# Attention with filler work placed by a table, and a first projection copied by ScalarE

## The chip, the cores and the metric

The kernel runs on all 8 cores of one Trainium2 chip. Each core computes one of the 8 batch elements by itself, and the cores exchange nothing. The metric is the time in microseconds (us) of the slowest core for one execution, lower being better. The engines of a core are TensorE (PE in the profile, with PEld for its weight loads), VectorE (DVE), ScalarE (ACT), GpSimd (POOL) and SyncE (SP). TensorE writes its results to PSUM, which the program divides into eight banks of 128 x 512 float32.

## The reference

Two layers, each a half-weighted SwiGLU, a mixer and another half-weighted SwiGLU, all with RMS norms and residual additions. The change touches only the mixer of layer 0, a banded attention with 16 heads of 64:

```
q, k, v = jnp.split(h @ w_in, 3, axis=-1)
q = rms_norm(q.reshape(b, nc, CHUNK, N_HEADS, HEAD_DIM), q_gain)
k = rms_norm(k.reshape(b, nc, CHUNK, N_HEADS, HEAD_DIM), k_gain)
scores = einsum('bnqhd,bnkhd->bnhqk', q, k_band) * HEAD_DIM ** -0.5
scores = where(valid, scores + bias, MASK_VALUE)
probs = softmax(scores)
out = einsum('bnhqk,bnkhd->bnqhd', probs, v_band).reshape(b, s, d)
return out @ w_out
```

Each chunk of 64 frames attends to itself and to the 8 chunks before it. A core has 2048 frames of width 1024.

## The kernel before

The activations lie transposed in on-chip memory: 8 row blocks of 128 channels by 2048 frames, the frames cut in 4 tiles (t) of 512. The program is six subprograms in a row: SwiGLU, attention, SwiGLU, SwiGLU, recurrent block, SwiGLU. Every engine has one queue, filled in the order in which the Python code records operations, and a small planner adds the semaphore waits that reads and writes need, per tile and per PSUM bank. So the order of the recorded calls is the order of the work, and an instruction that waits holds back all that was recorded after it on its engine.

**Pairs and steps.** Attention works on 8 pairs of heads (i = 0 to 7), a pair filling 128 channels. For a pair there are 28 steps: the tile t = 0 of queries meets 4 key blocks of 128, the tiles 1 to 3 meet 8 each, and a step spans 512, 384, 256 or 128 queries. `stage1(g)` computes the scores of step g for both heads into banks 0 and 1 or 2 and 3 (by turns), ScalarE takes the exponential of both into a buffer, and VectorE multiplies by the bias table and clears the corner outside of the band. `stage2(g - 2)` comes two steps later (LA = 2): four matmuls add values times probabilities in bank 4 and the row sums in bank 5. At the last step of a tile, ScalarE takes logarithm and exponential of bank 5, VectorE copies bank 4 and multiplies.

**Filler work.** Between stage1 and stage2 of the steps of pair i, the projections of pair i + 1 are put, since TensorE would have little to do otherwise. `proj_chunks` makes the list. `P1` is a projection of queries (`which` 0, bank 6) or keys (`which` 1, bank 7) of one tile: 8 matmuls of 512 columns in two halves of 4, then a copy to `raw` by VectorE (L672) and a square by GpSimd (L310). `P2` is the norm of a tile: two matmuls (`P2s`) sum the squares into banks 6 and 7, `P2f` takes one logarithm and one exponential over both banks (128 x 1024), and VectorE multiplies twice. `V` makes the values of two pairs for 128 frames: 8 matmuls of 256 columns into bank 6 or 7, then two casts by VectorE (L712). The list runs tile by tile: four halves of P1, up to two V, P2, then the other V. The loop over steps takes pieces from it by weight: each piece has a weight (0.87 or 0.6), each step has one by its columns (1.5 more at a tile's start), and pieces are taken while their share is not above that of the steps. What is left is issued at the next pair's first step. In pair 6 there are no V, and pair 7 has pieces of the output projection.

**First projection.** Pair 0's own projection overlaps the end of the SwiGLU before it. `seq0` lists 8 (tile, which) couples. For each of the first six, the sums of the one before (`after(x - 1)`) are issued first, into the same banks 0 to 3 that the projections use, then the whole P1. The rest follows with 16 V in banks 4 and 5, whose copies and casts are VectorE's.

`conv_bias` (two exponentials on ScalarE, a clear on VectorE, the next bias table's load on SP) comes at a pair's first step. Weights of a later pair are loaded from the GpSimd queue by `load_pair`.

Of the kernel before, what the change touches and what calls it, by code (L numbers as in the profile page):

```python
# [9 lines left out]
ALU = mybir.AluOpType  # L10
# [12 lines left out]
TAILJ = 20  # L23

ENGS = ("pe", "act", "dve", "pool", "sp")

class T:
    __slots__ = ("name", "last_w", "readers")
# [164 lines left out]
class Builder:  # L193
# [406 lines left out]
    def attention(self, n):  # L600
# [61 lines left out]
        def P1(p, t, which, bank, half=None):  # L662
            s = wsl(p)
            r = t % 2
            w = self.WA[s].rearrange("p (k m) -> p k m", k=8)
            tsl = slice(t * TT, (t + 1) * TT)
            for kc in (range(NCH) if half is None else range(4 * half, 4 * half + 4)):
                self.mm(bank, self.psum[bank], w[:, kc, which * 128:(which + 1) * 128], self.hT[:, kc, tsl],
                        kc == 0, kc == NCH - 1, [self.WA_t[s], self.h_t[kc][t]])
            if half == 0:  # L670
                return
            P.op("dve", lambda e: e.tensor_copy(out=raw[r][:, which, :], in_=self.psum[bank]),  # L672
                 reads=[self.ps_t[bank]], writes=[raw_t[r][which]])
            sqb, sqt = (E[2][:, which, :], sq0_t[which]) if p == 0 else (self.sq[which], self.sq_t[which])
            self.tt(sqb, raw[r][:, which, :], raw[r][:, which, :], ALU.mult,
                    [raw_t[r][which]], [sqt], eng="pool")

        def P2s(p, t, which, bank):
            sqb, sqt = (E[2][:, which, :], sq0_t[which]) if p == 0 else (self.sq[which], self.sq_t[which])
# [19 lines left out]
        def V(p, kt, bank):  # L699
            sa, sb = wsl(p), wsl(p + 1)  # L700
            lo, hi = min(sa, sb), max(sa, sb)
            d = hi - lo
            t = kt // 4
            ksl = slice(kt * 128, (kt + 1) * 128)
            for kc in range(NCH):
                self.mm(bank, self.psum[bank][:, 0:256], self.hT[:, kc, ksl],
                        WAall[:, lo:hi + 1:d, kc * 384 + 256:kc * 384 + 384], kc == 0, kc == NCH - 1,
                        [self.WA_t[sa], self.WA_t[sb], self.h_t[kc][t]])
            va, vb = p % NV, (p + 1) % NV
            order = (va, vb) if lo == sa else (vb, va)  # L710
            for j, sl in enumerate(order):
                P.op("dve", lambda e, j=j, sl=sl: e.tensor_copy(out=Vall[:, sl, kt, :], in_=self.psum[bank][:, j * 128:(j + 1) * 128]),  # L712
                     reads=[self.ps_t[bank]], writes=[v_t[sl][kt]])

        def proj_chunks(i):
            p = i + 1
            out = []
            vp, vk = None, []
            if i % 2 == 0 and i + 3 < 8:
                vp, vk = i + 2, list(range(0, 8))  # L720
            elif i % 2 == 1 and i + 2 < 8:
                vp, vk = i + 1, list(range(8, 16))
            nv = [0, 2, 3, 3]
            j = 0
            for t in range(NT):
                for which in range(2):
                    for half in range(2):
                        out.append((0.87, lambda t=t, which=which, half=half: P1(p, t, which, 6 + which, half)))
                mine = vk[j:j + nv[t]]
                j += nv[t]  # L730
                for kt in mine[0:2]:
                    out.append((0.87, lambda kt=kt: V(vp, kt, 6 + kt % 2)))
                out.append((0.6, lambda t=t: P2(p, t, 6)))
                for kt in mine[2:]:
                    out.append((0.87, lambda kt=kt: V(vp, kt, 7)))
            if p + 3 < 8:
                out.append((0.0, lambda: load_pair(p + 3)))
            return out

        seq0 = [(t, which) for t in range(NT) for which in range(2)]  # L740

        def after(x):
            t, which = seq0[x]
            P2s(0, t, which, 2 * (t % 2))
            if which == 1:
                P2f(0, t, 2 * (t % 2))

        for x in range(6):
            t, which = seq0[x]
            yield t  # L750
            if x == 0:
                load_pair(2)
            if x >= 1:
                after(x - 1)
            P1(0, t, which, 2 * (t % 2) + which)
        yield 99
        conv_bias(0)
        V(0, 0, 4)
        V(0, 1, 5)
        after(5)  # L760
        for kt in range(2, 8):
            V(0, kt, 4 + kt % 2)
        P1(0, 3, 0, 2)
        V(0, 8, 4)
        V(0, 9, 5)
        after(6)
        P1(0, 3, 1, 3)
        for kt in range(10, 14):
            V(0, kt, 4 + kt % 2)
        after(7)  # L770
        V(0, 14, 4)
        V(0, 15, 5)
        load_pair(3)

        out_w = [None] * 8
# [76 lines left out]
                self.tt(attnT[:, i, tsl], Osb, rsn, ALU.mult, [Osb_t, rsn_t], [at_t[i][t]])  # L852

        LA = 2
        fill = []
        done, total = 0.0, 0.0
        pend = []
        wgt = []
        for (t, kt, first, last) in seq:
            wgt.append(max(0.3, (min(TT * t + TT, 128 * kt + 640) - max(TT * t, 128 * kt)) / 512.0))  # L860
        for k in range(LA, ns):
            if seq[k - LA][2] and k > LA:
                wgt[k] += 1.5
        cum = [sum(wgt[:k + 1]) for k in range(ns)]
        for g in range(len(steps) + LA):
            i = g // ns
            k = g % ns
            if k == 0 and i < 8:
                while fill:
                    fill.pop(0)[1]()  # L870
                if i < 7:
                    conv_bias(i + 1)
            if g < len(steps):
                stage1(g)
            if k == LA and i < 8:
                if i < 7:
                    fill = proj_chunks(i)
                    total = sum(f[0] for f in fill)
                done = 0.0
                if i == 6:  # L880
                    for j in (0, 1, 2, 3, 6, 7):
                        load_out_w(j)
                if i == 7:
                    for j in (4, 5):
                        load_out_w(j)
            if i < 7:
                goal = total * (cum[k] - cum[LA - 1]) / (cum[ns - 1] - cum[LA - 1]) if k >= LA else 0.0
                while fill and done + fill[0][0] * 0.5 <= goal:
                    done += fill[0][0]
                    fill.pop(0)[1]()  # L890
            else:
                for _ in range(2):
                    if pend:
                        pend.pop(0)()
            if g >= LA:
                stage2(g - LA)
                i2, t2, kt2, first2, last2 = steps[g - LA]
                if i2 == 7 and last2 and t2 < 2:
                    for c in range(NCH):
                        for half in range(2):  # L900
                            pend.append(lambda t=t2, c=c, half=half: out_chunk(t, c, 6 + c % 2, half))
# [426 lines left out]
```

How the kernel before makes its waits and increments, by code:

```python
            def run(e, eng):  # L120
# [15 lines left out]
                    best = {}  # L136
                    for sem, val in waits:
                        k = id(sem)
                        if k not in best or best[k][1] < val:
                            best[k] = (sem, val)
                    waits = list(best.values())
                    embed = None
                    if waits and not op.is_dma:
                        embed = waits.pop()
                    for sem, val in waits:
                        eng.wait_ge(sem, val)
                    ins = op.fn(eng)
                    if embed is not None:
                        ins._wait_ge(embed[0], embed[1])
                    if op.is_dma:
                        ins.then_inc(dsem[op.dma_sem_id], 16)
                    elif op.needs_inc:
                        ins.then_inc(esem[e], 1)
                if e == "sp":
                    for op in final_wait_ops:
                        if waited_d[op.dma_sem_id] < op.dma_val:
                            eng.wait_ge(dsem[op.dma_sem_id], op.dma_val)
                            waited_d[op.dma_sem_id] = op.dma_val
```

## Time and profile before

| | us |
|---|---|
| three runs | 2743.55, 2738.2, 2742.05 (median 2742.05) |
| profiled execution, its own time | 2738.65 |
| its span, slowest core (core 4) | 2737.1 |
| spans of the eight cores | 2720.6 to 2737.1 |

The profile is one execution, seen on core 4; times count from the first instruction of that core. A row such as `PE ps L294 <- ACT arena L303` says that matmuls, all recorded at line 294, stood idle until an instruction of ScalarE, recorded at line 303, ended. Many lines are those of helpers (L294 matmul, L303 activation, L306 and L310 VectorE arithmetic, L310 on POOL the squares), so shapes tell what an instruction is. "Busy" of TensorE has its ends modelled. PEclk is the granted TensorE clock as a share of 2.4 GHz; half is 1.2 GHz. On this time axis attention runs from about 500 us to 990 us.

### The profile page before, as it was taken

The numbers are of one execution on the slowest core, as the hardware profiler recorded it, in microseconds if no ns is written. First come the engines' busy times: TensorE is split into PE (matmuls) and PEld (weight loads), VectorE is DVE, ScalarE is ACT, GpSimd is POOL, SyncE is SP. The second block draws the span as 40 slices with busy tenths as digits, with TensorE's granted clock in tenths as the row PEclk, the third lists the DMA queues.
The fourth block names the chain that finished last, engine by engine and source line by source line (L and its number), as shares of the span: only waits on it lengthen the run. The fifth ranks groups of instructions, "written<-read, shape, count | busy, mean of one in ns | idle before, by whom it ended". The sixth has DMA issues, their size and how long they took to land.

```text
span 2737.1 us, 30678 instructions; the slowest of 8 cores (2720.6 to 2737.1 us)
## 1 busy us (share of the span) xinstructions
PE 2567.1 (94%) x12224; PEld 1114.7 (41%) x12224; DVE 1179.1 (43%) x1851; ACT 789.9 (29%) x1141; POOL 347.9 (13%) x340
## 2 busy tenths in 40 slices
PE   6999999788888799999999999999978889999999
PEld 2444444333333234444444444444423334444444
DVE  4234234455555453423425243243567853424423
ACT  5110113255556542011014101102356632010010
POOL 0100000111111101000000100000048630000000
PEclk9999999899999899999999999999989999999999
DMA  6521310111001103231221412211111113222223
GB/s 151 85 38 25 54 28 15 27 32 16 16 16 21 30 1 61 37 54 28 34 35 16 74 27 43 45 29 28 20 21 20 18 27 61 40 50 32 34 35 119
DMA packets 56095, 105.85 MB, mean 39 GB/s; under 512 B 4624, under 2 KB 5776, under 8 KB 55952
## 3 DMA queue, kind: packets, MB, share of 16 engines
q0 software_dynamic: 44288, 83.90, 18.6%
q1 hardware_dynamic: 11664, 19.99, 2.5%
q8 instruction: 96, 1.57, 0.2%
q14 instruction: 47, 0.39, 0.0%
HBM read 179.37 MB, written 8.39 MB: 69 GB/s over the span
## 4 chain that ended last, share of the span: by engine, by line
PE 85%; DVE 6%; ACT 5%; POOL 2%; DMA 1%; issue 1%; SPq 0%; ACTq 0%; POOLq 0%; DVEq 0%
PE ps L294 85%; ACT arena L303 4%; DVE arena L306 3%; POOL arena L310 2%; DVE arena L310 1%; DMA arena<-xT 1%; DVE arena L317 1%; DVE arena L672 0%; SPq L332 0%; DVE arena L314 0%; DMA arena<-attn_wout 0%; ACT L303 0%; POOL arena L317 0%; DVE arena L850 0%; DMA arena<-lru_wout 0%
## 5 line engine op out<-in xcount | busy, mean ns | idle before, releaser
L294 PE MATMUL ps<-arena 128*128 128x512 bf16 (+6 forms) x12224 | 2567.1, 376 | 166.5 <-ACT arena L303 50.2
L294 PEld LDWEIGHTS ps<-arena 128*128 128x128 bf16 (+2 forms) x12224 | 1114.7, 100 | 1618.4 <-issue 222.3
L303 ACT ACTIVATE arena<-ps 128x512 bf16<-128x512 f32 (+5 forms) x680 | 444.9, 661 | 1698.3 <-PE ps L294 1653.7
L310 DVE TENSOR_TENSOR arena<-arena,ps 128x512 bf16<-128x512 bf16 x352 | 241.9, 688 | 951.6 <-PE ps L294 950.8
L306 DVE SCALAR_TENSOR_TENSOR arena<-ps,arena 128x512 f32<-128x512 f32 (+1 forms) x560 | 415.3, 742 | 222.6 <-PE ps L294 220.5
L303 ACT ACTIVATE arena<-arena 128x512 bf16<-128x512 f32 (+4 forms) x322 | 229.0, 742 | 160.2 <-PE ps L294 58.1
L310 POOL TENSOR_TENSOR arena<-arena 128x512 bf16<-128x512 f32 (+2 forms) x112 | 195.3, 1754 | 368.0 <-PE ps L294 258.5
L448 POOL DMA_DIRECT2D arena<-ffn_win x88 | 62.5, 710 | 1253.6 <-PE ps L294 1226.9
L306 DVE SCALAR_TENSOR_TENSOR arena<-arena,ps 128x512 bf16<-128x512 f32 x192 | 133.9, 742 | 33.7 <-ACT ps L303 33.7
L310 DVE TENSOR_TENSOR arena<-arena 128x512 bf16<-128x512 bf16 (+3 forms) x188 | 86.6, 473 | 91.9 <-ACT arena L303 90.0
L454 POOL DMA_DIRECT2D arena<-ffn_wout x88 | 48.5, 557 | 396.7 <-PE ps L294 396.1
L306 DVE SCALAR_TENSOR_TENSOR arena<-arena 128x512 bf16<-128x512 f32 (+3 forms) x88 | 57.2, 681 | 67.2 <-ACT arena L303 66.4
L303 ACT ACT_TABLE_LOAD x51 | 65.4, 1283 | 7.3 <-PE ps L294 3.5
L310 DVE TENSOR_TENSOR arena<-ps,arena 128x512 f32<-128x512 f32 x64 | 43.3, 689 | 51.7 <-PE ps L294 51.3
L303 ACT ACTIVATE arena<-ps,arena 128x512 f32<-128x512 f32 x64 | 43.8, 688 | 63.2 <-PE ps L294 63.2
L672 DVE COPY arena<-ps 128x512 f32<-128x512 f32 x64 | 43.4, 687 | 20.4 <-PE ps L294 19.6
L317 DVE TENSOR_SCALAR arena<-ps,arena 128x1024 f32<-128x1024 f32 x16 | 21.4, 1339 | 36.7 <-PE ps L294 23.1
L314 DVE TENSOR_SCALAR arena<-arena 128x1024 f32<-128x1024 f32 (+3 forms) x24 | 29.4, 1224 | 17.5 <-ACT arena L303 16.3
L712 DVE CAST arena<-ps 128x128 bf16<-128x128 f32 x128 | 29.9, 275 | 12.7 <-PE ps L294 12.1
L1081 DVE TENSOR_TENSOR_SCAN arena<-arena 128x1024 f32<-128x1024 f32 x8 | 31.8, 3975 | 0.8
L832 DVE MEMSET arena<- 64x128 bf16 x96 | 15.8, 165 | 36.3 <-ACT arena L303 33.8
L317 POOL TENSOR_SCALAR arena<-arena 128x1024 f32<-128x1024 f32 x16 | 21.1, 1319 | 60.3 <-ACT arena L303 60.2
(20 smaller groups left out, 87.6 us busy)
## 6 DMA issues: line engine op xcount, KB each, us to landing
arena<-ffn_win POOLq DMA_DIRECT2D x88, 512.0 KB, 5.3
arena<-ffn_wout POOLq DMA_DIRECT2D x88, 256.0 KB, 6.0
arena<-xT SPq DMA_DIRECT2D x32, 256.0 KB, 13.1
outT<-arena SPq DMA_DIRECT2D x32, 256.0 KB, 2.9
arena<-attn_win POOLq DMA_DIRECT2D x8, 768.0 KB, 7.8
arena<-lru_win POOLq DMA_DIRECT2D x8, 512.0 KB, 5.3
arena<-bias_tab SPq DMA_DIRECT2D x8, 256.0 KB, 4.3
arena<-attn_wout POOLq DMA_DIRECT2D x8, 256.0 KB, 4.8
```

The source lines that it names most:

```text
L294: self.P.op("pe", lambda e: e.matmul(out_ap, lhsT, rhs, start=start, stop=stop), reads=reads, writes=[self.ps_t[bank]])
L303: self.P.op("act", lambda e: e.activation(out=out, in_=in_, func=func, **kw), reads=reads, writes=writes)
L306: self.P.op("dve", lambda e: e.scalar_tensor_tensor(out=out, in0=in0, scalar=scalar, in1=in1, op0=op0, op1=op1), reads=reads, writes=writes)
L310: self.P.op(eng, lambda e: e.tensor_tensor(out=out, in0=in0, in1=in1, op=op), reads=reads, writes=writes)
L314: self.P.op(eng, lambda e: e.tensor_scalar(out=out, in0=in0, scalar1=s1, scalar2=None, op0=op0), reads=reads, writes=writes)
L317: self.P.op(eng, lambda e: e.tensor_scalar(out=out, in0=in0, scalar1=s1, scalar2=s2, op0=op0, op1=op1), reads=reads, writes=writes)
L448: P.dma("pool", lambda e: e.dma_start(out=self.WA[s][:, 0:2048], in_=self.fwin_d[fi, j], max_dma_last_dim=4096), self.WA_sem[s], writes=[s ...
L454: P.dma("pool", lambda e, s=s, j=j: e.dma_start(out=self.WBall[:, s, :], in_=self.fwout_d[fi, j * 128:(j + 1) * 128, :], max_dma_last_dim= ...
L672: P.op("dve", lambda e: e.tensor_copy(out=raw[r][:, which, :], in_=self.psum[bank]), reads=[self.ps_t[bank]], writes=[raw_t[r][which]])
L712: P.op("dve", lambda e, j=j, sl=sl: e.tensor_copy(out=Vall[:, sl, kt, :], in_=self.psum[bank][:, j * 128:(j + 1) * 128]), reads=[self.ps_t ...
L832: P.op("dve", lambda e: e.memset(E[r][0:64, :, 576 - lo:640 - lo], 0.0), reads=Ex_t[r], writes=et)
L1081: P.op("dve", lambda e: e.tensor_tensor_scan(out=hb, data0=tha, data1=thx, initial=carry[:, 0:1], op0=ALU.mult, op1=ALU.add), reads=[that, ...
```

## The change

Four edits. First, `PLAN` takes the place of the weights: a table with a row for even and one for odd pairs, with 28 entries each. An entry lists the pieces issued at that step between stage1 and stage2. Letters: `q21` is the second half of P1 for the queries of tile 2, `k` the same for keys; `s` and `t` are the sum matmul of queries and of keys of a tile; `f` and `g` are the rest of their norms; `v37` is V number 3 in bank 7. Second, the norm is cut in two: `F` takes the logarithm in place in its bank, the exponential from the bank to `rs`, and multiplies, each over 512 columns, for queries and keys apart. So a pair has 40 pieces: 16 halves, 8 sums, 8 norm parts, 8 V. Third, in the first projection the copies and casts go from VectorE to ScalarE, sums go to banks 4 and 5, V to banks 6 and 7, and the sums of couple x - 2 are issued between the two halves of couple x. Last, `load_pair` is at the start of the following pair's first step, where it had been the last piece of the list.

```diff
--- before.py
+++ after.py
@@ -23,6 +23,23 @@
 TAILJ = 20
 
 ENGS = ("pe", "act", "dve", "pool", "sp")
+
+PLAN = [
+    ["", "k00 q00", "q01 k01", "",
+     "", "s0 t0 f0 g0", "q10 q11 k10", "k11",
+     "", "", "s1 t1 f1", "g1",
+     "q20 q21", "", "k20 k21 v06", "",
+     "", "s2 v17 f2", "t2 g2 v46", "",
+     "", "v37", "q30 q31 k30 k31", "v26",
+     "", "s3 v77 f3", "", "v56 t3 v66 g3",],
+    ["", "q00 q01 k00 k01", "s0 f0", "",
+     "t0 q10 q11 g0", "", "k10 k11", "",
+     "", "", "s1 t1 f1 g1", "",
+     "q20 q21", "v17", "v06 k20", "",
+     "k21", "s2 f2", "", "v27 v36",
+     "", "t2 v46", "q30 g2 q31", "k30 k31",
+     "s3 v77 f3", "v57", "", "t3 v66 g3",],
+]
 
 class T:
     __slots__ = ("name", "last_w", "readers")
@@ -669,11 +686,13 @@
                         kc == 0, kc == NCH - 1, [self.WA_t[s], self.h_t[kc][t]])
             if half == 0:
                 return
-            P.op("dve", lambda e: e.tensor_copy(out=raw[r][:, which, :], in_=self.psum[bank]),
-                 reads=[self.ps_t[bank]], writes=[raw_t[r][which]])
+            if p == 0:
+                self.act(raw[r][:, which, :], self.psum[bank], AF.Copy, [self.ps_t[bank]], [raw_t[r][which]])
+            else:
+                P.op("dve", lambda e: e.tensor_copy(out=raw[r][:, which, :], in_=self.psum[bank]),
+                     reads=[self.ps_t[bank]], writes=[raw_t[r][which]])
             sqb, sqt = (E[2][:, which, :], sq0_t[which]) if p == 0 else (self.sq[which], self.sq_t[which])
-            self.tt(sqb, raw[r][:, which, :], raw[r][:, which, :], ALU.mult,
-                    [raw_t[r][which]], [sqt], eng="pool")
+            self.tt(sqb, raw[r][:, which, :], raw[r][:, which, :], ALU.mult, [raw_t[r][which]], [sqt], eng="pool")
 
         def P2s(p, t, which, bank):
             sqb, sqt = (E[2][:, which, :], sq0_t[which]) if p == 0 else (self.sq[which], self.sq_t[which])
@@ -709,67 +728,75 @@
             va, vb = p % NV, (p + 1) % NV
             order = (va, vb) if lo == sa else (vb, va)
             for j, sl in enumerate(order):
-                P.op("dve", lambda e, j=j, sl=sl: e.tensor_copy(out=Vall[:, sl, kt, :], in_=self.psum[bank][:, j * 128:(j + 1) * 128]),
-                     reads=[self.ps_t[bank]], writes=[v_t[sl][kt]])
-
-        def proj_chunks(i):
+                if p == 0:
+                    self.act(Vall[:, sl, kt, :], self.psum[bank][:, j * 128:(j + 1) * 128], AF.Copy, [self.ps_t[bank]], [v_t[sl][kt]])
+                else:
+                    P.op("dve", lambda e, j=j, sl=sl: e.tensor_copy(out=Vall[:, sl, kt, :], in_=self.psum[bank][:, j * 128:(j + 1) * 128]),
+                         reads=[self.ps_t[bank]], writes=[v_t[sl][kt]])
+
+        def F(p, t, which):
+            r = t % 2
+            bank = 6 + which
+            tsl = slice(t * TT, (t + 1) * TT)
+            self.act(self.psum[bank], self.psum[bank], AF.Ln, [self.ps_t[bank]], [self.ps_t[bank]], scale=1.0, bias=64.0 * EPS)
+            self.act(self.rs[which], self.psum[bank], AF.Exp, [self.ps_t[bank]], [self.rs_t[which]], scale=-0.5)
+            dst, dst_t, sc, sc_t = (qT, q_t, qg, self.cv_t) if which == 0 else (kT, k_t, kg8, self.dc_t)
+            self.stt(dst[p % 2][:, tsl], raw[r][:, which, :], sc, self.rs[which], ALU.mult, ALU.mult,
+                     [raw_t[r][which], self.rs_t[which], sc_t], [dst_t[p % 2][t]])
+
+        def token(i, tok):
             p = i + 1
-            out = []
-            vp, vk = None, []
-            if i % 2 == 0 and i + 3 < 8:
-                vp, vk = i + 2, list(range(0, 8))
-            elif i % 2 == 1 and i + 2 < 8:
-                vp, vk = i + 1, list(range(8, 16))
-            nv = [0, 2, 3, 3]
-            j = 0
-            for t in range(NT):
-                for which in range(2):
-                    for half in range(2):
-                        out.append((0.87, lambda t=t, which=which, half=half: P1(p, t, which, 6 + which, half)))
-                mine = vk[j:j + nv[t]]
-                j += nv[t]
-                for kt in mine[0:2]:
-                    out.append((0.87, lambda kt=kt: V(vp, kt, 6 + kt % 2)))
-                out.append((0.6, lambda t=t: P2(p, t, 6)))
-                for kt in mine[2:]:
-                    out.append((0.87, lambda kt=kt: V(vp, kt, 7)))
-            if p + 3 < 8:
-                out.append((0.0, lambda: load_pair(p + 3)))
-            return out
+            kind = tok[0]
+            if kind in "qk":
+                which = "qk".index(kind)
+                P1(p, int(tok[1]), which, 6 + which, int(tok[2]))
+            elif kind in "st":
+                which = "st".index(kind)
+                P2s(p, int(tok[1]), which, 6)
+            elif kind in "fg":
+                F(p, int(tok[1]), "fg".index(kind))
+            elif kind == "v":
+                n_, b_ = int(tok[1]), int(tok[2])
+                if i % 2 == 0 and i + 3 < 8:
+                    V(i + 2, n_, b_)
+                elif i % 2 == 1 and i + 2 < 8:
+                    V(i + 1, 8 + n_, b_)
 
         seq0 = [(t, which) for t in range(NT) for which in range(2)]
 
         def after(x):
             t, which = seq0[x]
-            P2s(0, t, which, 2 * (t % 2))
+            P2s(0, t, which, 4)
             if which == 1:
-                P2f(0, t, 2 * (t % 2))
+                P2f(0, t, 4)
 
         for x in range(6):
             t, which = seq0[x]
             yield t
             if x == 0:
                 load_pair(2)
-            if x >= 1:
-                after(x - 1)
-            P1(0, t, which, 2 * (t % 2) + which)
+            P1(0, t, which, 2 * (t % 2) + which, 0)
+            if x >= 2:
+                after(x - 2)
+            P1(0, t, which, 2 * (t % 2) + which, 1)
         yield 99
+        V(0, 0, 6)
+        after(4)
+        V(0, 1, 7)
+        V(0, 2, 6)
+        after(5)
         conv_bias(0)
-        V(0, 0, 4)
-        V(0, 1, 5)
-        after(5)
-        for kt in range(2, 8):
-            V(0, kt, 4 + kt % 2)
+        for kt in range(3, 6):
+            V(0, kt, 6 + kt % 2)
         P1(0, 3, 0, 2)
-        V(0, 8, 4)
-        V(0, 9, 5)
+        P1(0, 3, 1, 3)
+        V(0, 6, 6)
         after(6)
-        P1(0, 3, 1, 3)
-        for kt in range(10, 14):
-            V(0, kt, 4 + kt % 2)
+        V(0, 7, 7)
+        V(0, 8, 6)
         after(7)
-        V(0, 14, 4)
-        V(0, 15, 5)
+        for kt in range(9, 16):
+            V(0, kt, 6 + kt % 2)
         load_pair(3)
 
         out_w = [None] * 8
@@ -852,31 +879,17 @@
                 self.tt(attnT[:, i, tsl], Osb, rsn, ALU.mult, [Osb_t, rsn_t], [at_t[i][t]])
 
         LA = 2
-        fill = []
-        done, total = 0.0, 0.0
         pend = []
-        wgt = []
-        for (t, kt, first, last) in seq:
-            wgt.append(max(0.3, (min(TT * t + TT, 128 * kt + 640) - max(TT * t, 128 * kt)) / 512.0))
-        for k in range(LA, ns):
-            if seq[k - LA][2] and k > LA:
-                wgt[k] += 1.5
-        cum = [sum(wgt[:k + 1]) for k in range(ns)]
         for g in range(len(steps) + LA):
             i = g // ns
             k = g % ns
-            if k == 0 and i < 8:
-                while fill:
-                    fill.pop(0)[1]()
-                if i < 7:
-                    conv_bias(i + 1)
+            if k == 0 and 0 < i < 8 and i + 3 < 8:
+                load_pair(i + 3)
+            if k == 0 and i < 7:
+                conv_bias(i + 1)
             if g < len(steps):
                 stage1(g)
             if k == LA and i < 8:
-                if i < 7:
-                    fill = proj_chunks(i)
-                    total = sum(f[0] for f in fill)
-                done = 0.0
                 if i == 6:
                     for j in (0, 1, 2, 3, 6, 7):
                         load_out_w(j)
@@ -884,10 +897,8 @@
                     for j in (4, 5):
                         load_out_w(j)
             if i < 7:
-                goal = total * (cum[k] - cum[LA - 1]) / (cum[ns - 1] - cum[LA - 1]) if k >= LA else 0.0
-                while fill and done + fill[0][0] * 0.5 <= goal:
-                    done += fill[0][0]
-                    fill.pop(0)[1]()
+                for tok in PLAN[i % 2][k].split():
+                    token(i, tok)
             else:
                 for _ in range(2):
                     if pend:
```

## Rows read from the trace of the kernel before

**Rows 1.** the profile's page, its first engine row and the chain that ended last

```profile
PE 2567.1 (94%) x12224; PEld 1114.7 (41%) x12224; DVE 1179.1 (43%) x1851; ACT 789.9 (29%) x1141; POOL 347.9 (13%) x340
PE 85%; DVE 6%; ACT 5%; POOL 2%; DMA 1%; issue 1%; SPq 0%; ACTq 0%; POOLq 0%; DVEq 0%
```

**Rows 2.** windows: length; PE, PEld, DVE, ACT, POOL busy (count); granted clock

```profile
503.00:557.70 54.70, 38.71 (x206) 21.12 (x204) 23.77 (x56) 12.75 (x16) 9.12 (x9) 0.84 0.03 6
...
665.70:720.30 54.60, 46.69 (x304) 18.87 (x304) 28.95 (x73) 32.53 (x47) 9.02 (x9) 0.94 0.22 35
...
884.20:943.00 58.80, 43.68 (x242) 13.49 (x242) 27.97 (x59) 34.28 (x48) 11.05 (x13) 0.84 0.12 19
960.00:1700.00 740.00, 735.34 (x3451) 326.13 (x3450) 280.57 (x424) 149.24 (x243) 44.34 (x71) 1.00 0.23 38
```

**Rows 3.** waits of the matmuls, 560 to 890 us (total, times, longest)

```profile
PE ps L294 <- ACT arena L303: 24.2, 24, 1.2
PE ps L294 <- POOL arena L310: 8.0, 6, 1.4
PE ps L294 <- DVE arena L672: 7.5, 6, 1.2
PE ps L294 <- DVE arena L850: 4.0, 6, 1.5
PE ps L294 <- DVE arena L310: 3.2, 6, 0.5
PE ps L294 <- DVE arena L712: 1.3, 6, 0.2
```

**Rows 4.** timeline of TensorE in pair 1 (start, us, ..., idle before)

```profile
622.37 0.38 PE L294 MATMUL ps<-arena 128*128 128x512 bf16 x1 [1.37 <-POOL arena L310]
...
655.87 5.42 PE L294 MATMUL ps<-arena 128*128 128x256 bf16 x42 [1.25 <-DVE arena L672]
```

**Rows 5.** windows of one us in pair 1

```profile
621.00:622.00 1.00, 0.01 (x1) 0.00 (x0) 0.73 (x2) 0.97 (x3) 0.81 (x1) 1.00 0.00 0
...
623.00:624.00 1.00, 0.14 (x1) 0.11 (x2) 0.11 (x1) 0.97 (x2) 0.00 (x0) 1.00 0.00 0
624.00:625.00 1.00, 1.00 (x3) 0.30 (x2) 0.07 (x1) 0.90 (x1) 0.00 (x0) 0.50 0.00 0
```

**Rows 6.** ScalarE's groups by shape in pair 2, 665.7 to 720.3 us

```profile
L303 ACT ACTIVATE arena<-ps 128x1024 bf16<-128x1024 f32 x8 | 8.0, 1019 | 2.8 <-PE ps L294 2.0 <-DVE arena L310 0.5 <-DVE arena L832 0.3
...
L303 ACT ACTIVATE arena<-arena 128x1024 f32<-128x1024 f32 x4 | 4.2, 1058 | 0.1
...
L303 ACT ACTIVATE arena<-ps 128x1024 f32<-128x1024 f32 x4 | 4.1, 1021 | 0.3 <-PE ps L294 0.2
L303 ACT ACTIVATE arena<-ps 128x256 bf16<-128x256 f32 x7 | 2.7, 379 | 4.3 <-PE ps L294 3.2 <-DVE arena L310 1.1
...
L303 ACT ACTIVATE arena<-ps 128x512 f32<-128x512 f32 x4 | 2.4, 598 | 2.1 <-PE ps L294 2.1
```

**Rows 7.** timeline of TensorE in the first projection (first and fifth of five gaps)

```profile
506.61 2.10 PE L294 MATMUL ps<-arena 128*128 128x512 bf16 x9 [1.56 <-POOL arena L310]
...
528.22 5.54 PE L294 MATMUL ps<-arena 128*128 128x512 bf16 x25 [2.68 <-POOL arena L310]
```

**Rows 8.** waits of the matmuls, 884.2 to 943 us

```profile
PE ps L294 <- POOL arena L310: 7.2, 3, 3.1
```

**Rows 9.** timeline of GpSimd in pair 1, a square

```profile
621.18 1.04 POOL L310 TENSOR_TENSOR arena<-arena 128x512 bf16<-128x512 f32 x1 [1.45 <-PE ps L294]
```

**Rows 10.** VectorE's groups by shape in pair 2

```profile
L672 DVE COPY arena<-ps 128x512 f32<-128x512 f32 x8 | 5.4, 687 | 1.4 <-PE ps L294 1.3
...
L712 DVE CAST arena<-ps 128x128 bf16<-128x128 f32 x16 | 3.7, 272 | 1.2 <-PE ps L294 1.1
```

**Rows 11.** timeline of ScalarE before the first projection

```profile
488.41 1.28 ACT L303 ACT_TABLE_LOAD   x1
489.70 0.60 ACT L303 ACTIVATE arena<-ps 128x512 f32<-128x512 f32 x1
```


## Prediction

> **What bounds the kernel now.** I read the page first. TensorE is busy 94% of the span and holds 85% of the chain that ended last [rows 1], so time can only come from TensorE's idle time or its clock. The windows by stage then say where both are [rows 2]. In the SwiGLU from 960 us TensorE is busy 735.34 of 740 us at a granted clock of 1.00: nothing to win. In attention, one steady pair takes 54.6 us with 46.69 busy, so 7.9 idle, at clock 0.94. Pair 0 takes 53.3 us and the other five to 884.2 us all take 54.6 or 54.7 with the same counts (304 matmuls), so one pair stands for six. The first projection (503 to 557.7 us) has 38.71 busy of 54.7 at 0.84, and pair 6 with the head of pair 7 (884.2 to 943) has 43.68 busy of 58.8 at 0.84.
>
> The waits say what each idle piece is [rows 3]. Between 560 and 890 us they sum to 24.2 + 8.0 + 7.5 + 4.0 + 3.2 + 1.3 = 48.2 us, or 8.0 a pair, and come in fixed numbers: four a pair on ScalarE, one each on the others. The timeline gives the place [rows 4]. The first tile's sums follow its last projection at once and wait 1.37 us for the square of GpSimd. Right behind, the next projection wants bank 6 and waits some 1.0 us (24.2 by 24 [rows 3]) until the logarithm over both banks has read it. Later a V waits 1.25 us for the copy out of its bank. These are waits of order, not of load: ScalarE is busy 32.53, VectorE 28.95 and GpSimd 9.02 of 54.6 us [rows 2].
>
> Last, the clock. It falls to 1.2 GHz (0.50) twice a pair, both times behind the pair's start with its short steps and waits, the second time at 624 us; from 621 to 624 us TensorE was nearly idle (0.01 and 0.14 busy in two of the three microseconds) [rows 5]. A mean of 0.94 over 54.6 us is 0.06 x 54.6 = 3.3 us of lost full-speed work. So a steady pair is 46.7 - 3.3 = 43.4 us of work at 2.4 GHz, 3.3 of clock and 7.9 idle.
>
> **The change, part by part.**
>
> *The table in pairs 0 to 5.* It removes and adds no matmul. What moves: sums now come one to five steps behind their projection, and the norm parts one or more steps before the next use of their bank. I walked the queues with the rows' durations. The norm was 1.02 + 1.06 = 2.08 us of ScalarE for a tile; now it is four instructions of 512 columns at 0.60 (the nearest row, 598 ns, reads a bank and writes on-chip memory; in place no row shows) = 2.4, so 0.3 more a tile, 1.3 a pair [rows 6]. ScalarE then has 33.8 us of a pair, below TensorE's 43.4, but every exponential of scores queued behind an F comes 1.2 us later. The cover is LA = 2: stage2 wants it two steps later, with the filler of two steps between (9 matmuls of 512 columns take 2.10 us to their end [rows 7], so a half projection, or a V with its 8 of 256, is some 0.9).
>
> Even row, step 5 ("s0 t0 f0 g0") is the tight place. The scores of step 4 end at 0 on my count, those of step 5 at 0.9; their exponentials (1.02 each) end at 1.0 and 2.0, f0 at 3.2, g0 at 4.4. TensorE has the two sums, stage2 of step 3 and the scores of step 6 until about 1.9, and the next piece, q10, wants bank 6: a wait of 1.3 us. I found only 0.3 more there (t0 for the square of k) and no other in the even row: s1, s2, s3 and the V that follow have at least one step between. In the odd row, f0 and g0 are at steps 2 and 4, and my count gives 0.4 us at s0 and 0.4 at the copy of bank 4. At the pair's boundary the old order had the norm (2.08), the two bias exponentials (1.0) and the step's exponential in one run before the second step's scores; now g3 alone (1.2) is there, behind a V. So 1.6 and 0.8 us by the walk; semaphore delays and VectorE's own queue are not in it, so I take 2.2 idle a pair. From below it can't be less than 0, from above it is today's 7.9 if every wait only changes its name.
>
> With no idle piece above 1.4 us in a row, the stretch that pulled the clock down is gone: waits such as the 1.25 us at 655.87 [rows 4], alone in their surroundings, were not followed by a fall. I take 0.6 us for clock losses left, between 0 and today's 3.3. A pair is then 43.4 + 2.2 + 0.6 = 46.2 us, a gain of 8.4, or 50 for six; the bounds are 0 and 11.2 a pair.
>
> *Pair 6.* Work at full clock in the 58.8 us: the lost clock is 0.16 x 58.8 x 0.74 (the busy share) = 7.0, so 43.7 - 7.0 = 36.7, and 15.1 idle, of which 7.2 are three waits for the square (one 3.1 us long) because no V stands between P1 and P2 [rows 8]. The table keeps the distance in steps though the V are gone, so these go. But ScalarE has 34.28 + 1.3 = 35.6 us there, nearly TensorE's own work, so steps without filler run at ScalarE's pace, above all 16 to 21. I take 9 idle and 5 of clock: 50.7, a gain of 8, taken as 7; bounds 0 and 15.
>
> *First projection.* Five gaps, all but one for the square, 11.0 us in sum (1.56, 2.22, 2.41, 2.12, 2.68; first and last in [rows 7]), come from `after(x - 1)` ahead of P1(x). With `after(x - 2)` between halves the square has 1.73 + 0.9 = 2.6 us, against a copy of 0.6 and a square of 1.04 [rows 9], so four of them go; the one behind a P2f waits some 0.2 us as the copy is now queued on ScalarE behind 2.08 us of norm. A copy on ScalarE costs 0.60 for 0.69 on VectorE [rows 6, 10]; a cast of 128 columns shows on no ScalarE row: between 0 and the 0.38 of 256 columns, I take 0.27, for 0.27 on VectorE. New is that V's casts stand behind norm and bias exponentials on ScalarE (1.02 + 1.06 + 1.0 = 3.1 us) while only two banks serve V (1.76 us of TensorE): 1.3 to 1.9 us of waiting after after(5), and about 0.9 after after(7). Work at full clock is 38.7 - 0.16 x 54.7 x 0.71 = 32.5; with 5.5 idle and 4 of clock it is 42.0, a gain of 12.7, taken as 10 because this part has most unseen operations; bounds -3 (all gaps stay, and the 2.8 of V are added) and 17.
>
> The Trainium skill (ScalarE: Activation LUTs, Table sets) says that cheap functions, copy among them, are in every table set. By it the copies need no table load, which is the sum above. The trace bears it out only for its kin: after the load at 488.41 us, logarithm, exponential and square run mixed without another [rows 11]. If copy wanted a set of its own, each switch would cost the 1.28 us of that row, and with ten groups of copies between the norms, so 20 switches, the first projection would be 26 us longer and the time about 2700.
>
> *Loads.* `load_pair` stays at the pair boundary; first use of its weights is 14 steps later, over 20 us, so nothing hangs on it. SP has only the bias table, which is asked for at the same step.
>
> **Sum.** 50 + 7 + 10 = 67 us off the profiled execution's own 2738.65, which is 2672. That execution lies 3.4 below the median of the runs shown, so the forecast is about 2674.
>
> **The rivals.**
>
> *A, the forecast:* the waits go and the clock follows. 2655 to 2695. Chance 0.58.
>
> *B, half of it:* the waits go by half, since VectorE's queue (multiply behind exponential, then the raw copy behind that) moves later what my walk has in time, and the clock falls as often as now. 4 a pair, 6 in the first projection, 3 in pair 6: 24 + 6 + 3 = 33, so 2708; span 2695 to 2725. For it: ScalarE and VectorE are each busy more than half of a pair [rows 2], and each works strictly in the recorded order. Against it: the slack of two steps. 0.21.
>
> *C, new waits for old:* bank 6 and 7 are held through F's exponential, where they were free after the logarithm, and every tile pays as step 5 does. Four tiles by 1.3 and a longer start leave 1 us a pair or less: 2735 to 2745, so 2738. 0.08.
>
> *D, the other side, ScalarE's queue:* eight F a pair put 1.2 us each ahead of a score exponential. If the next stage2 has no filler to cover them, TensorE pays 8 x 1.2 = 9.6 a pair where 7.9 went, 1.7 x 6 = 10, and 3 in the first projection: 2755. It decides from the point where more than six of the eight F are uncovered; the even row has two in a step at step 5 only, and my walk finds one uncovered. 0.10.
>
> *E, a limit on dense work:* a denser TensorE is granted less. With the clock staying where it is and only the idle gone, 5.7 x 6 + 5 + 7 = 46 remain, 2696. The Trainium skill (TensorE: Matmul & The Clock Gate, Part 1) speaks against the change here: it says that once three cores of a die run dense matmuls the die is held to 13/16. By it the densest stretches could not have full clock. This case's trace disagrees: 99% busy at 1.00 for 740 us, with eight cores at work [rows 2]. 0.03.
>
> **How the numbers follow.** The likeliest is A, 2674. Leaving out the slower side and most of C, which is 2 in 10, the range is 2652 to 2722; its lower end is 90 off the profiled time (with the 3.4 of the median), nine tenths of what the upper bounds give together (67 + 15 + 17 = 99). About 0.2% (5.5 us) is what a measurement can tell from no change. Faster by more: A, B, E and a little of C, 0.85. Same: 0.06. Slower: D and the tail of C, 0.09.
>
> **What would show it.** Right: a steady pair of 45 to 48 us with under 3.5 idle, its clock at 0.98 or more; no wait for POOL in it; a wait on ScalarE of 1.0 to 1.6 us in even pairs only, before q10; 503 to the first score in 40 to 46 us with no new ACT_TABLE_LOAD; and the stretches after attention as before. Wrong: pairs above 50 us, waits of VectorE's copies that my walk has in time, or a clock that still falls behind each pair's start.

## The result and the profile after

The changed kernel takes 2652.5 us (median), the kernel before 2742.05, so 89.5 us less; the ratio is 0.9677, 95% interval 0.9655 to 0.9699, or 3.2% less. Forecast were 2674 with a range of 2652 to 2722. At times one die ran slower whatever the kernel; every number here is from undisturbed runs.

The page of the kernel after, its engine row and its chain, for [rows 1]:

```profile
PE 2530.7 (95%) x12224; PEld 1113.0 (42%) x12224; DVE 1175.0 (44%) x1811; ACT 800.3 (30%) x1237; POOL 349.4 (13%) x340
PE 89%; DVE 6%; ACT 2%; DMA 1%; issue 1%; POOL 1%; SPq 0%; ACTq 0%; DVEq 0%; POOLq 0%
```

The same matmuls (x12224) are 36 us less busy, and idle time fell by 50. The windows of the stages, for [rows 2] (length; busy us of the engines; granted clock). The first is the first projection, then pairs 0 and 1, pairs 0 to 5 together, and pair 6:

```profile
498.00:543.00 45.00, 41.55 (x254) 23.79 (x253) 20.57 (x31) 26.51 (x62) 9.52 (x9) 1.00 0.11 23
543.00:586.10 43.10, 41.23 (x298) 18.30 (x297) 29.08 (x70) 31.99 (x53) 9.01 (x9) 1.00 0.25 44
586.10:631.40 45.30, 42.95 (x306) 18.83 (x305) 30.18 (x73) 32.26 (x55) 9.23 (x9) 1.00 0.02 7
...
543.00:809.80 266.80, 254.49 (x1819) 112.33 (x1818) 180.06 (x430) 195.17 (x323) 54.93 (x54) 1.00 0.13 24
809.80:862.00 52.20, 42.03 (x268) 14.67 (x265) 29.14 (x63) 35.92 (x60) 12.91 (x16) 0.89 0.20 29
```

Six pairs that took 326.5 us (557.7 to 884.2) take 266.8, or 44.5 each, and the clock is 1.00 where it was 0.94. The waits of the matmuls in these 266.8 us, for [rows 3]:

```profile
PE ps L311 <- DVE arena L734: 5.2, 12, 0.8
PE ps L311 <- DVE arena L877: 2.9, 6, 0.6
PE ps L311 <- ACT arena L320: 2.5, 3, 1.5
PE ps L311 <- POOL arena L327: 1.3, 2, 0.7
```

That is 11.9 us where there were 48.2, and the 24 waits for ScalarE became three. The largest part of what is left (5.2) is for VectorE's casts of V out of their bank (L734): in odd pairs k20 and q30 come close behind a V in their bank (0.43 and 0.78 us), and in each two pairs a V does so twice (0.37 and 0.15). In TensorE's timeline of the pairs the longest stretches without a gap were 16.6 us; now one is 32.7, and two things stand out (start, us, ..., idle before), for [rows 4, 7]:

```profile
526.74 9.30 PE L311 MATMUL ps<-arena 128*128 128x256 bf16 x66 [1.84 <-ACT arena L320]
536.95 12.26 PE L311 MATMUL ps<-arena 128*128 128x256 bf16 x88 [0.91 <-ACT arena L320]
550.71 32.72 PE L311 MATMUL ps<-arena 128*128 128x512 bf16 x236 [1.50 <-ACT arena L320]
...
639.93 32.72 PE L311 MATMUL ps<-arena 128*128 128x512 bf16 x236 [0.51 <-ACT arena L320]
...
820.97 0.58 PE L311 MATMUL ps<-arena 128*128 128x512 bf16 x1 [5.19 <-POOL arena L327]
```

The first two are the V of the first projection, the next two are q10 behind step 5 of even pairs, and the last is new: 5.19 us in pair 6. GpSimd's queue tells why:

```profile
812.12 1.59 POOL L812 DMA_DIRECT2D arena<-attn_wout  x3 [6.75 <-PE ps L311]
819.23 0.53 POOL L812 DMA_DIRECT2D arena<-attn_wout  x1 [5.52 <-DMA arena<-attn_wout]
819.77 2.05 POOL L327 TENSOR_TENSOR arena<-arena 128x512 bf16<-128x512 f32 x2
```

Row block 7 of the output weights goes to another part of the buffer of row block 6, but the planner tracks that buffer as one. So its load waits 5.52 us for the landing of block 6, and two squares stand behind it. Behind the idle time the clock is 0.50 from 820 to 826 us. Of the unseen operations, the logarithm in place takes what I assumed (first line, 545 to 803 us), and so does the cast (second, 498 to 543 us):

```profile
L320 ACT ACTIVATE ps<-ps 128x512 f32<-128x512 f32 x46 | 27.4, 595 | 2.2 <-PE ps L311 2.2
...
L320 ACT ACTIVATE arena<-ps 128x128 bf16<-128x128 f32 x32 | 6.8, 276 | 5.4 <-PE ps L311 5.4
```

The time axis of a trace starts with its core's first instruction, and what lies ahead of attention differs by some us between cores: the ScalarE table load just ahead of the first projection is at 488.41 us in the trace before [rows 11] and 4.5 later in this one. So stages are best counted between marks inside one trace. The marks here are that load, the weight load of the first score (first line after, second before), and VectorE's copies of bank 4 at the end of pairs 5 and 6:

```profile
492.95 1.28 ACT L320 ACT_TABLE_LOAD   x1
...
541.42 0.12 PEld L311 LDWEIGHTS ps<-arena 64*128 64x128 bf16 x4 [0.21 <-issue]
...
555.39 0.11 PEld L294 LDWEIGHTS ps<-arena 64*128 64x128 bf16 x4 [0.21 <-issue]
```

| us between the marks | before | after | e1 | e2 | e3 | e10 |
|---|---|---|---|---|---|---|
| load to first score | 67.0 | 48.5 | 67.0 | 49.1 | 49.1 | 48.5 |
| first score to end of pair 5 | 330.7 | 270.3 | 272.3 | 330.6 | 308.1 | 302.7 |
| end of pair 5 to end of pair 6 | 56.2 | 45.7 | 46.0 | 55.9 | 47.9 | 47.7 |

From before to after that is 18.5 + 60.4 + 10.5 = 89.4 us, all of the measured difference, and behind pair 6 the two traces are as long to 1.2 us (1794.8 and 1793.6). The first row before differs by core, from 65.6 (core 7) to 68.1 (core 2), while after it is 48.5 on all of cores 0, 2, 3, 5 and 7, so the 18.5 stands for some 17 to 20. The other columns are the runs of the next section.

### The profile page after: what moved, and what is told of

Its sections match the earlier page's. It is cut to its first block, busy times and chain, and to the rows that moved or that the text cites. A ratio compares the mean times of both kernels' runs of the same rounds, so it can differ in the third digit from the quotient of the medians.

```text
span 2651.0 us, 30732 instructions; the slowest of 8 cores (2646.7 to 2651.0 us)
## 1 busy us (share of the span) xinstructions
PE 2530.7 (95%) x12224; PEld 1113.0 (42%) x12224; DVE 1175.0 (44%) x1811; ACT 800.3 (30%) x1237; POOL 349.4 (13%) x340
## 4 chain that ended last, share of the span: by engine, by line
PE 89%; DVE 6%; ACT 2%; DMA 1%; issue 1%; POOL 1%; SPq 0%; ACTq 0%; DVEq 0%; POOLq 0%
PE ps L311 89%; DVE arena L323 4%; ACT arena L320 2%; DVE arena L334 1%; DMA arena<-ffn_win 1%; DVE arena L327 0%; POOL arena L327 0%; DMA arena<-xT 0%; DVE arena L331 0%; DMA arena<-lru_wout 0%; DMA arena<-attn_wout 0%; SPq L349 0%; DVE arena L877 0%; DVE arena L734 0%; ACT ps L320 0%
## 5 line engine op out<-in xcount | busy, mean ns | idle before, releaser
L311 PE MATMUL ps<-arena 128*128 128x512 bf16 (+6 forms) x12224 | 2530.7, 373 | 116.7 <-ACT arena L320 26.4
L320 ACT ACTIVATE arena<-ps 128x512 bf16<-128x512 f32 (+6 forms) x748 | 457.2, 626 | 1602.2 <-PE ps L311 1580.0
L320 ACT ACTIVATE arena<-arena 128x512 bf16<-128x512 f32 (+4 forms) x294 | 199.0, 710 | 154.3 <-PE ps L311 58.2
L327 DVE TENSOR_TENSOR arena<-arena 128x512 bf16<-128x512 bf16 (+3 forms) x188 | 92.6, 505 | 55.9 <-ACT arena L320 52.2
L320 ACT ACTIVATE ps<-ps 128x512 f32<-128x512 f32 x56 | 33.4, 596 | 6.6 <-PE ps L311 6.6
L1092 DVE TENSOR_TENSOR_SCAN arena<-arena 128x1024 f32<-128x1024 f32 x8 | 31.8, 3977 | 0.8
L1087 DVE TENSOR_TENSOR_SCAN arena<-arena 128x1024 f32<-128x1024 f32 x8 | 25.0, 3122 | 5.7 <-POOL arena L327 5.7
```

The lines of the kernel that those rows point to most:

```text
L311: self.P.op("pe", lambda e: e.matmul(out_ap, lhsT, rhs, start=start, stop=stop), reads=reads, writes=[self.ps_t[bank]])
L320: self.P.op("act", lambda e: e.activation(out=out, in_=in_, func=func, **kw), reads=reads, writes=writes)
L327: self.P.op(eng, lambda e: e.tensor_tensor(out=out, in0=in0, in1=in1, op=op), reads=reads, writes=writes)
L1087: P.op("dve", lambda e: e.tensor_tensor_scan(out=hb, data0=tha, data1=thx, initial=0.0, op0=ALU.mult, op1=ALU.add), reads=[that, thxt], wr ...
L1092: P.op("dve", lambda e: e.tensor_tensor_scan(out=hb, data0=tha, data1=thx, initial=carry[:, 0:1], op0=ALU.mult, op1=ALU.add), reads=[that, ...
```

## The experiments

**The two halves by themselves.** First the table with the first projection as before (`e1_table_only`), then the new first projection with the old list (`e2_first_projection_only`).

```diff
# e1, on the kernel after
-            if p == 0: self.act(raw..., AF.Copy, ...)      # V's casts likewise
+            P.op("dve", ... tensor_copy ...)
-            P2s(0, t, which, 4)
+            P2s(0, t, which, 2 * (t % 2))
...  # the loop over seq0 and the V after it as in the kernel before
# e2: the reverse, on the kernel before
```

> The table and the split norm, with the first projection as it was (copies and casts on VectorE, sums in banks 0 to 3, V in 4 and 5, sums of the couple before ahead of each projection). The theory: the parts add up, so the 13.8 us of the first projection stay and the 60.6 of pairs 0 to 5 and 10.5 of pair 6 go: about 2668 us, ratio to before 0.973 to 0.975, a steady pair 44.6 us at clock 1.00. Rival: the pairs are this fast only because VectorE starts them without a backlog and TensorE enters them at full clock; then the ratio is 0.98 or more and the first pairs take over 47 us.

> Only the first projection is changed; the list, its weights and the joint norm stay. The theory: 13.8 us less, about 2728 us, ratio 0.995, pairs still 54.6 us at clock 0.94. [...]

Measured: e1 2672.0 us, ratio 0.9756 (0.9737 to 0.9776), 67 less than before. e2 2720.9, ratio 0.9936 (0.9916 to 0.9955), 18 less. The sum, 85, is the whole within the intervals, so the parts are nearly independent. Of e1's rival 2 us are true: with the casts on VectorE the six pairs take 272.3 us in place of 270.3, in e1 as in `e7_casts_on_vector` below. In e2 the pairs kept their length and a clock of 0.94 (542 to 868 us). e2 gave more than the 13.8 I had read off the start of pair 0, because I had compared two time axes that are 4.5 us apart; between marks it is 17.9 in e2 and 18.5 in the changed kernel.

**The cut of the norm.** Once taken back in the changed kernel (`e3_table_joint_norm`), once alone in the kernel before (`e4_list_split_norm`), once cut but kept together (`e10_cut_together`).

```diff
# e3, in token(), on the kernel after
-                P2s(p, int(tok[1]), which, 6)
+                if which == 1: P2(p, int(tok[1]), 6)       # s, f, g: nothing
# e4, in P2, on the kernel before
-            P2f(p, t, bank)
+            F(p, t, 0); F(p, t, 1)
# e10: as e3, with both P2s, F(p, t, 0), F(p, t, 1) at t
```

> The changed kernel, but the norm of a tile is in one piece again, as before: both sums, one logarithm and one exponential over 1024 columns and both multiplies are issued at the table's entry t. Theory (the distance in steps does it, not the cut): ScalarE has 0.3 us less a tile, and a wait of about 1 us comes only where a q follows t at once (odd pairs, tile 0): 2650 to 2668 us, ratio to before 0.967 to 0.973. Rival (the cut of the norm does it, since long logarithms no longer stand before the scores' exponentials): over 2690 us, ratio above 0.98.

> The kernel before with the norm cut in two as in the change, all else as before. Theory: bank 6 is free after logarithm and exponential of 512 (1.2 us) where it was free after one logarithm of 1024 (1.02), so the wait grows by 0.2 us for each of 28 tiles and ScalarE by 0.3: 2742 to 2752 us, ratio 1.000 to 1.004. Rival (the cut does it): under 2720 us, ratio below 0.992.

> As the run with the joint norm (both sums and the whole norm at the table's entry t), but with the norm cut in two: logarithm and exponential of 512 for queries, then for keys, back to back. It parts the cut from the distance. If the 37 us that the joint norm cost come from the pieces now standing together at t (bank 6 asked for right behind), cutting them gives little: 2680 to 2700 us, ratio to before 0.978 to 0.985. If the long instructions do it, it is near the changed kernel: under 2665 us, ratio below 0.972.

Measured: e3 2690.3 us, a single run and so without an interval, some 38 more than the changed kernel; e4 ratio 1.0008 (0.9997 to 1.0019); e10 2686.4 in its profiled execution, with a wide ratio, 0.9856 (0.9784 to 0.9927). On e3 my theory, 2650 to 2668, missed, and the number lies at the edge of the rival's (over 2690). But what the rival says, that the cut itself does it, fell by e4 and e10: cutting gives nothing in the old list, and 4 to 5 us with the pieces together (the six pairs take 302.7 us in e10, 308.1 in e3). What counts is that a cut norm can be put apart: that is 32 us of the six pairs (302.7 to 270.3), while the table with an uncut norm gives 23 (330.7 to 308.1). A window and the waits of e3 from 560 to 800 us:

```profile
560.00:800.00 240.00, 210.78 (x1436) 90.20 (x1434) 136.95 (x342) 150.66 (x216) 43.06 (x42) 0.96 0.10 20
```

```profile
PE ps L311 <- ACT arena L320: 17.2, 14, 1.9
PE ps L311 <- DVE arena L734: 5.6, 10, 0.7
```

Fourteen waits for ScalarE of up to 1.9 us are back (the changed kernel has two, 1.0 us in all, in this stretch), and with them falls of the clock (0.96 for 1.00). By the table's order, a projection or V right behind t asks for bank 6 before the long logarithm has read it.

**Does idle time pull the clock down?** `e5_idle_filled` puts matmuls that nobody reads into two waits of each pair of the kernel before.

```diff
+            if k == 2 and i < 7: dummy(4)                  # ahead of stage1
+        def dummy(n): n matmuls, ones x hT[:, 0, 0:512], into bank 6
         def P2(p, t, bank):
+            if t == 0: dummy(5)
```

> The kernel before, with extra matmuls (ones times 512 columns of the input, into bank 6, never read) inside two waits of each pair: 5 before the sums of tile 0, where TensorE waits 1.4 us for the square, and 4 before the scores of the third step, where it waits 1.2 us. They do no useful work and lengthen no chain by more than 0.3 us. If idle time is what pulls the clock down, one or both falls of a pair go and with them 1.7 to 3.4 us a pair: 2720 to 2732 us, ratio 0.992 to 0.997, clock of a pair 0.97 to 1.00. Rival: the falls belong to the kind of work at the pair's start (short steps, 64 rows); then the clock stays 0.94 and the time is the same or up to 4 us longer (ratio 1.000 to 1.002).

Measured: 2722.8 us, ratio 0.9936 (0.9917 to 0.9956): 17 us less with 63 more matmuls. A window of exactly one pair, and the wait for the square in two pairs one after the other:

```profile
671.22:722.90 51.68, 44.82 (x309) 19.01 (x314) 29.43 (x73) 32.60 (x47) 9.01 (x9) 1.00 0.13 21
```

```profile
671.22 0.38 PE L294 MATMUL ps<-arena 128*128 128x512 bf16 x1 [0.32 <-POOL arena L310]
...
722.90 0.38 PE L294 MATMUL ps<-arena 128*128 128x512 bf16 x1 [0.44 <-POOL arena L310]
```

A pair is 51.68 us in place of 54.6, and both falls are gone although the short steps stand where they were. So it is the idle time before a fall that does it. Without the nine added matmuls (1.9 us, at the 735.34 us for 3451 of [rows 2]) the pair has 42.9 us of work, or up to 43.8 since four of its 313 matmuls are missing from the trace, where it had 46.69. So the falls cost 2.9 to 3.8 us a pair; the prediction read 3.3 from 0.94. The rival (the kind of work) fell.

**How near is ScalarE's queue?** `e8_exp_twice` does each norm part's exponential twice.

```diff
             self.act(self.rs[which], self.psum[bank], AF.Exp, ..., scale=-0.5)
+            self.act(self.rs[which], self.psum[bank], AF.Exp, ..., scale=-0.5)
```

> The changed kernel with the exponential of each norm part done twice (same result): 0.60 us more of ScalarE, 8 times a pair in 7 pairs, 33.6 us in all. It asks how much slack the queue has. Theory (norm parts are covered by filler, LA = 2): most of it is hidden, up to 12 us longer, ratio to before 0.968 to 0.973. Rival (ScalarE's queue is on the path, as in my case of the other side): 25 us or more, ratio above 0.977.

Measured: 2672.6 us, ratio 0.9755 (0.9738 to 0.9771), some 20 more than the changed kernel of the 33.6 added. Between both expectations: the queue has slack for the work as it is, and of 0.6 us more a norm part it hides about two fifths. Its waits from 560 to 800 us:

```profile
PE ps L311 <- ACT arena L320: 10.5, 19, 1.0
PE ps L311 <- POOL arena L327: 4.1, 8, 1.4
```

**Mending what is left.** `e6_late_load` moves one load; `e7_casts_on_vector` takes the casts of the first projection back to VectorE; `e11_four_banks` gives its V four banks; `e12_both_mends` is e6 and e11.

```diff
# e6
-                    for j in (0, 1, 2, 3, 6, 7):
+                    for j in (0, 1, 2, 3, 6):
+            if i == 6 and k == 19: load_out_w(7)
# e7, in V
-                if p == 0: self.act(Vall..., AF.Copy, ...)
+                P.op("dve", ... tensor_copy ...)
# e11, after the loop over seq0: banks of the V
-        6, 7, 6 | 7, 6, 7 | 6, 7, 6 | 7, 6, 7, 6, 7, 6, 7
+        6, 7, 0 | 1, 6, 7 | 0, 1, 6 | 7, 0, 1, 6, 7, 6, 7
```

> The changed kernel with one load moved: row block 7 of the output weights, which shares a buffer with row block 6 and so waits on the GpSimd queue for that load's landing, ahead of two squares in pair 6, is issued at step 19 of pair 6. Theory: the 5.2 us wait of TensorE for the square goes, and the fall of the clock behind it: 5 to 7 us less than the changed kernel, ratio to before 0.965 against 0.968. Rival: the four loads before it, which wait for TensorE, hold the squares too; then at most 2 us.

> The changed kernel with the casts of the first projection's V on VectorE again (banks 6 and 7, order and ScalarE's copies of queries and keys stay). Theory: the waits of V for its bank (1.84 and 0.91 us, both for ScalarE, whose queue has the norm and the bias exponentials ahead of the casts) go, 2.5 us less than the changed kernel, ratio to before 0.967. Rival: the casts then stand behind VectorE's multiplies, which wait for the same norm, and the waits only change their engine: 0 to 1 us less.

> The changed kernel with the V of the first projection going round banks 6, 7, 0 and 1 in place of 6 and 7; casts stay on ScalarE. Theory: the waits of 1.84 and 0.91 us (a third V asks for a bank whose cast stands behind the norm and the bias exponentials) are for want of a bank, so two more banks take them away: 2.5 to 4 us less than the changed kernel, ratio to before about 0.967 against 0.968. Rival: ScalarE's backlog is handed on to the first scores and their wait grows by as much: no change.

> The changed kernel with the four banks and with the late load of row block 7, which alone took some 7 us. If the two are independent, 9 to 11 us less than the changed kernel: 2642 to 2644 us, ratio to before 0.964 to 0.965. If the first gives nothing, 2646 us, ratio 0.9655.

e6: 2645.7 and 2646.3 us, ratio 0.9657 (0.9634 to 0.9681), 5 to 7 less than the changed kernel as expected (the intervals of the ratios overlap, so it is the trace that shows it): the wait is 1.19 us where it was 5.19, and pair 6 takes 39.0 between its marks for 45.7, so 6.7 less:

```profile
814.11 0.88 PE L311 MATMUL ps<-arena 128*128 128x512 bf16 x7 [1.19 <-POOL arena L327]
```

e7: 2660.0 us, ratio 0.9708 (0.9689 to 0.9727), 7 more. The intervals just overlap, but the trace shows it: from table load to first score are 55.7 us for 48.5. My theory fell, and the rival was too mild. VectorE's casts stand behind multiplies that wait for the whole norm, the V wait longer, and behind the first of these waits the clock is 0.50 (527 to 531 us):

```profile
527.50 12.25 PE L311 MATMUL ps<-arena 128*128 128x256 bf16 x65 [2.79 <-DVE arena L734]
...
542.11 5.03 PE L311 MATMUL ps<-arena 128*128 128x256 bf16 x44 [2.37 <-DVE arena L734]
```

So in the first projection ScalarE is the better place for the casts, which was part of the change and which I had priced as even. e11: the wait of 1.84 is 0.57 in the trace and that of 0.91 is 0.28, while q10's stays:

```profile
521.27 15.89 PE L311 MATMUL ps<-arena 128*128 128x256 bf16 x125 [0.57 <-ACT arena L320]
...
545.89 14.28 PE L311 MATMUL ps<-arena 128*128 128x512 bf16 x90 [1.50 <-ACT arena L320]
```

The ratio, 0.9677 (0.9663 to 0.9692), is the changed kernel's, since 2 or 3 us are below what it tells. The marks tell more: from table load to first score are 45.4 us for 48.5, and the six pairs behind take 270.3 in both. So 3.1 us are gained, as expected, and nothing is handed on to the pairs (the first mark reads 45.4 on cores 0, 2, 5 and 7 of that trace). e12: 2642.9 us, ratio 0.9654 (0.9640 to 0.9668), beside 2649.6 for e11 and 2737.1 for the kernel before on the same chip. It has both gains between its marks (45.4 and 39.0 us) and is the fastest version here, by median some 10 us below the changed kernel, though its interval still touches that one's.

## Why the prediction was right, and where it was off

The mechanism was right in the main, and the time 21 us too high: the result lies at the very edge of the range. Every term of the sum was too small: 60.4 us for 50 in the six pairs, 18.5 for 10 in the first projection, 10.5 for 7 in pair 6. (The sum as written also gives 2675, not 2674.) Of my signs of being right, the pair (44.5 for 45 to 48) and the first projection (36.2 for 40 to 46) came out shorter still.

*The pairs.* Forecast 46.2 us: 43.4 work, 2.2 idle, 0.6 clock. Measured 44.5: 42.4 busy, 2.05 idle, clock 1.00. The idle is right in size, which is partly luck, and half right in kind: of the waits I walked, q10 behind step 5 is there (1.50 in pair 0, but 0.51 in pairs 2 and 4, for 1.3), the one of t0 for the square (0.67 in pairs 2 and 4, for 0.3, though by my own signs no wait for POOL was to be left) and the one at the copy of bank 4 (0.6 for 0.4); the other half is waits for VectorE's casts of V, which I had left out of the walk and covered by a lump of 1.0. The 0.6 of clock was too careful: e5 shows that the falls hang on the idle time. For the last 1.0 I have no cause: e5's pair at full clock has 42.9 to 43.8 us of work by the old list, about the 43.4 of the forecast, so the new order counts 0.5 to 1.4 less busy for the same matmuls. Busy ends are modelled, and short waits may hide in them; no run shows it.

*The first projection* was the term sized worst: taken as 10, worked out as 12.7, bounded at 17, and measured at 18 (e2) to 18.5, above its own bound. Idle was 3.4 (0.32 + 0.31 + 1.84 + 0.91) for 5.5, with both V waits where and as long as I had them. But I kept 4 us of clock, of which none was lost (1.00 from 498 to 543 us), and then took 2.7 off for unseen operations, which cost what their neighbours do. The 32.5 of work with 3.4 idle is 35.9, which is what was measured (54.7 - 18.5 = 36.2).

*Pair 6* gained 10.5 for 7 (45.7 us from pair 5's last copy of bank 4 to its own, 56.2 before), in spite of a wait that I missed. I wrote that nothing hangs on the loads and looked at `load_pair` alone. The load of row block 7 waited as long before (5.61 us), but no matmul waited for it:

```profile
891.66 0.54 POOL L785 DMA_DIRECT2D arena<-attn_wout  x1 [5.61 <-DMA arena<-attn_wout]
893.24 1.04 POOL L310 TENSOR_TENSOR arena<-arena 128x512 bf16<-128x512 f32 x1 [1.05 <-DVE arena L672]
897.10 1.04 POOL L310 TENSOR_TENSOR arena<-arena 128x512 bf16<-128x512 f32 x1 [2.82 <-DVE arena L672]
```

GpSimd was free again at 892.2 us and idle until the copies by VectorE were there; the second square is the one that the 3.1 us wait of [rows 8] ended with. The table asks for the squares earlier, so that they now stand behind the load, and e6 shows what that costs: 6.7 us.

*The rivals.* B and C are refuted by the clock of 1.00 and the count of waits. D is refuted by the 2.5 us of waits for ScalarE (and e4, with the same eight F a pair in the old list, is no slower than before), though e8 shows the queue near: 0.6 us more a norm part cost 20 us. E: 266.8 us at 95% busy ran at 1.00. So what the Trainium skill says of a limit on dense work (TensorE: Matmul & The Clock Gate, Part 1) is not seen here either. The profile's page counts `ACT_TABLE_LOAD` x51 before and after, so no copy needed a load. The rule of the Trainium skill that copy is in every table set (ScalarE: Activation LUTs, Table sets) agrees with that.

## What to carry to other kernels

Where one engine is the bound and fillers hide its waits, look at what each filler piece asks for: separate a chain such as projection, copy, square, sum, norm by other pieces, so that no piece asks for a bank or a result of the piece just before. Count short waits twice, since enough of them together took the clock down here, and nine useless matmuls a pair paid for themselves in the old list (e5). After reordering, look at every in-order queue that the moved work now stands in, the DMA queue first. And compare stages of two traces between marks inside each, not by their time axes.

## What was not expected of the hardware

VectorE and GpSimd seem to slow each other where both read on-chip memory; no run here tests it. In the first projection, two multiplies of 128x512 on VectorE take 2.24 us beside GpSimd's squares, where two of the same shape with no square beside them take 1.42 (third line), and two squares take 2.48 us, where two take 2.08 at 636.32 us. At 521.01 us the multiplies again take 2.24, but the square beside them its usual 1.04.

```profile
516.58 2.24 DVE L323 SCALAR_TENSOR_TENSOR arena<-arena 128x512 bf16<-128x512 f32 x2 [0.28 <-ACT arena L320]
517.23 2.48 POOL L327 TENSOR_TENSOR arena<-arena 128x512 bf16<-128x512 f32 x2 [2.10 <-PE ps L311]
...
525.45 1.42 DVE L323 SCALAR_TENSOR_TENSOR arena<-arena 128x512 bf16<-128x512 f32 x2 [2.19 <-ACT arena L320]
```
